# Key blocks of 32 on column tiles for two products of a gated scan

## What is computed

```python
def step(S, xs):                      # per chunk of 64 tokens
    qc, kc, vc, bc = xs               # b: cumulative log of the forget gate f
    diff = bc[:, :, :, None, :] - bc[:, :, None, :, :]
    diff = jnp.where(causal[None, None, :, :, None], diff, -jnp.inf)
    A = jnp.einsum('bhtd,bhsd,bhtsd->bhts', qc, kc, jnp.exp(diff))
    o = (jnp.einsum('bhts,bhsv->bhtv', A, vc)
         + jnp.einsum('bhtd,bhdv->bhtv', qc * jnp.exp(bc), S))
    ...
```

## Time and profile before

| | before |
|---|---|
| median of three runs | 1464.66 us |
| the profiled execution | 1463.35 us |
| its span, first to last instruction | 1461.5 us |
| TensorE busy (matmuls) | 1430.2 us, 98% |
| VectorE busy | 873.5 us, 60% |
| ScalarE busy | 574.4 us, 39% |
| GpSimd busy | 0.2 us |
| DMA | 158.31 MB, 33% of 16 engines' span |

### The profile page before, as it was taken

One profiled execution on the slowest core, in us unless ns is written; L12 is line 12 of the kernel. 1 busy time (PEld: TensorE's weight loads), 2 busy tenths in 40 slices (PEclk: granted clock), 3 DMA queues, 4 the chain that ended last, 5 costly groups with the idle time before them and its releaser, 6 DMA issues.

```text
span 1461.5 us, 18543 instructions
## 1 busy us (share of the span) xinstructions
PE 1430.2 (98%) x7204; PEld 1194.5 (82%) x7204; DVE 873.5 (60%) x1720; ACT 574.4 (39%) x1075; POOL 0.2 (0%) x4
## 2 busy tenths in 40 slices
PE   4999999999999999999999999999999999999998
PEld 3788888988888888888888888888888888888886
DVE  7887776544333335756467434424778787787645
ACT  5423355422232334533333333423445544555441
POOL 0000000000000000000000000000000000000000
PEclk9999999999999999999999999999999999999999
DMA  8646542353333234123223333332222222222221
GB/s 331 225 170 222 180 137 74 126 202 92 96 101 96 92 101 144 32 99 117 85 87 107 99 98 101 101 96 77 73 73 68 63 73 73 73 73 61 84 72 59
DMA packets 43863, 158.31 MB, mean 108 GB/s; under 512 B 4864, under 2 KB 5248, under 8 KB 43776
## 3 DMA queue, kind: packets, MB, share of 16 engines
q1 hardware_dynamic: 43776, 157.12, 33.0%
HBM read 155.00 MB, written 2.10 MB: 107 GB/s over the span
## 4 chain that ended last, share of the span: by engine, by line
PE 95%; DVE 3%; DMA 1%; ACT 1%; issue 0%; SPq 0%; ACTq 0%; DVEq 0%
PE PS L498 29%; PE PS L500 29%; PE PS L499 29%; PE PS L782 1%; PE PS L834 1%; PE PS L793 1%; PE PS L494 1%; PE PS L838 1%; PE PS L828 1%; DVE RAW L951 1%; DMA X<-in_x 1%; PE PS L853 1%; PE PS L814 0%; DMA RAW<-in_ada 0%; DVE Z L951 0%
## 5 line engine op out<-in xcount | busy, mean ns | idle before, releaser
L498 PE MATMUL PS<-HH,WH 128*128 128x512 f32 (+1 forms) x1088 | 430.7, 396 | 0.0
L500 PE MATMUL PS<-HH,WL 128*128 128x512 f32 (+1 forms) x1088 | 418.4, 385 | 0.0
L499 PE MATMUL PS<-HL,WH 128*128 128x512 f32 (+1 forms) x1088 | 417.0, 383 | 0.0
L987 DVE TENSOR_TENSOR WL<-RAW,WH 128x1024 fp32r<-128x1024 f32 x219 | 266.1, 1219 | 70.3 <-ACT WH L1695 70.1
L1695 ACT ACTIVATE WH<-RAW 128x1024 fp32r<-128x1024 f32 x219 | 230.6, 1056 | 171.7 <-PE PS L500 138.0
L500 PEld LDWEIGHTS PS<-HH,WL 128*128 128x128 f32 x1088 | 204.4, 188 | 42.1
L498 PEld LDWEIGHTS PS<-HH,WH 128*128 128x128 f32 x1088 | 204.7, 188 | 36.9
L499 PEld LDWEIGHTS PS<-HL,WH 128*128 128x128 f32 x1088 | 205.0, 188 | 36.0
L498 PE MATMUL PS<-WH,ZH 128*128 128x512 f32 x400 | 155.9, 390 | 0.0
L500 PE MATMUL PS<-WH,ZL 128*128 128x512 f32 x400 | 155.6, 389 | 0.0
L499 PE MATMUL PS<-WL,ZH 128*128 128x512 f32 x400 | 155.6, 389 | 0.0
(11 more groups left out here) (262 smaller groups left out, 1764.8 us busy)
## 6 DMA issues: line engine op xcount, KB each, us to landing
RAW<-in_w_fc SPq DMA_DIRECT2D x64, 512.0 KB, 3.6
RAW<-in_hgrn_in SPq DMA_DIRECT2D x64, 512.0 KB, 3.5
RAW<-in_ada SPq DMA_DIRECT2D x43, 512.0 KB, 4.4
RAW<-in_pool_in SPq DMA_DIRECT2D x40, 512.0 KB, 3.6
RAW<-in_w_in SPq DMA_DIRECT2D x27, 512.0 KB, 4.5
RAW<-in_pool_out SPq DMA_DIRECT2D x16, 512.0 KB, 3.6
RAW<-in_hgrn_out SPq DMA_DIRECT2D x16, 512.0 KB, 3.5
RAW<-in_w_out SPq DMA_DIRECT2D x8, 512.0 KB, 3.8
```

Source lines behind the costliest of these rows:

```text
L498: e.matmul(out, wh, xh, start=first, stop=False)
L499: e.matmul(out, wh, xl, start=False, stop=False)
L500: return e.matmul(out, wl, xh, start=False, stop=last)
L987: e.tensor_tensor(lo, raw(i), hi.bitcast(F32), ALU.subtract).then_inc(taken.sem, taken(i))
```

## The change

The products of lines 782 and 793 are cut into 16 groups of 32 keys. Each group g is multiplied with the queries of its own 32 tokens alone, and its output goes to the partitions 32 (g mod 4) to 32 (g mod 4) + 31, that is to one of four column tiles of TensorE. For levels 0 and 8 the queries of a group stand together in t.qp, 32 and then 16, in all 48 columns, and go to columns 64 g to 64 g + 47 of the pair of banks; for level 16 there are 16 queries to a group. t.qp keeps its size of 768 columns, but is ordered by group. The counts of elements that VectorE handles stay; masks and their contents stay; the semaphore of bank 3 is raised at group 7, that of bank 4 at the last.

```diff
-        QP = [sb(f"QP{i}", [128, 4, 192]) for i in range(2)]
+        QP = [sb(f"QP{i}", [128, 16 * 48]) for i in range(2)]
...
-                for i, c in enumerate(blocks):
-                    m = e.matmul(PAIR[:, 256 * i:256 * i + 192], t.f[:, c], t.qp[:, i, :], start=True, stop=True)
-                    if i == 1:
+                for g in range(16):
+                    r = 32 * (g % 4)
+                    m = e.matmul(PAIR[r:r + 32, 64 * g:64 * g + 48], t.f[:, 32 * g:32 * g + 32],
+                                 t.qp[:, 48 * g:48 * g + 48], start=True, stop=True)
+                    if g == 7:
                         m.then_inc(banks.full[3], banks.fill(("level", h, 0), 3))
...
-                for i, c in enumerate(blocks):
-                    m = e.matmul(PS[b][:, 64 * i:64 * i + 64].rearrange("p (n l) -> p n l", l=16), t.k[:, c],
-                                 halves(t.q[:, c], 16)[1], start=True, stop=True)
+                for g in range(16):
+                    r = 32 * (g % 4)
+                    m = e.matmul(PS[b][r:r + 32, 16 * g:16 * g + 16], t.k[:, 32 * g:32 * g + 32],
+                                 t.q[:, 32 * g + 16:32 * g + 32], start=True, stop=True)
...
                 (q0, q1), (w0, w1), (i0, i1) = (
-                    [v.rearrange("p (i n) l -> p i n l", i=4) for v in halves(x, 4)]
+                    [v.rearrange("p (g n) l -> p g n l", g=16) for v in halves(x, 4)]
                     for x in (t.q, W[:, :], IW[:, :]))
-                p4 = t.qp[:, :, 0:128].rearrange("p i (n a l) -> p i n a l", a=2, l=4)
+                qp = t.qp.rearrange("p (g c) -> p g c", c=48)
+                p4 = qp[:, :, 0:32].rearrange("p g (n a l) -> p g n a l", a=2, l=4)
...
-                    return x.rearrange("p (i n o) -> p i n o", i=4, o=1).broadcast_to([128, 4, 8, 8])
-
-                p8 = t.qp[:, :, 0:128].rearrange("p i (n a l) -> p i n a l", a=2, l=8)
-                qv = t.q.rearrange("p (i n a l) -> p i n a l", i=4, a=2, l=8)
+                    return x.rearrange("p (g n o) -> p g n o", g=16, o=1).broadcast_to([128, 16, 2, 8])
+
+                p8 = qp[:, :, 0:32].rearrange("p g (n a l) -> p g n a l", a=2, l=8)
+                qv = t.q.rearrange("p (g n a l) -> p g n a l", g=16, a=2, l=8)
                 e.wait_ge(own.sem, own.of("q8", h))
-                e.tensor_tensor(t.qp[:, :, 128:192].rearrange("p i (n l) -> p i n l", l=8),
+                e.tensor_tensor(qp[:, :, 32:48].rearrange("p g (n l) -> p g n l", l=8),
                                 p8[:, :, :, 1, :], by_pair(t.q8), ALU.mult).then_inc(scaled.sem, scaled(h, 8))
...
-                e.copy_predicated(t.diag, MSK[:, 0:512].rearrange("p (i t) -> p i t", i=4),
-                                  four[:, :, 0:128]).then_inc(banks.free[3], 1)
+                e.copy_predicated(t.A.rearrange("p (g l) -> p g l", g=16),
+                                  MSK[:, 0:512].rearrange("p (g l) -> p g l", g=16),
+                                  pair[:, :, 0:32]).then_inc(banks.free[3], 1)
...
-                    MSK[:, 512:768].rearrange("p (i n l) -> p i n l", i=4, l=8),
-                    four[:, :, 128:192].rearrange("p i (n l) -> p i n l", l=8)).then_inc(banks.free[4], 1)
+                    MSK[:, 512:768].rearrange("p (g n l) -> p g n l", g=16, l=8),
+                    pair[:, :, 32:48].rearrange("p g (n l) -> p g n l", l=8)).then_inc(banks.free[4], 1)
```

More of the change, by code:

```diff
@@ L1546, in mixing @@
                 t = Head(h)
-                four = PAIR[:, :].rearrange("p (i t) -> p i t", i=4)
+                pair = PAIR[:, :].rearrange("p (g c) -> p g c", c=64)
                 b = level_bank(h, 16)
@@ L1550, in mixing @@
                 e.wait_ge(*banks.made(("level", h, 8)))
-                e.copy_predicated(t.diag, MSK[:, 0:512].rearrange("p (i t) -> p i t", i=4),
-                                  four[:, :, 0:128]).then_inc(banks.free[3], 1)
+                e.copy_predicated(t.A.rearrange("p (g l) -> p g l", g=16),
+                                  MSK[:, 0:512].rearrange("p (g l) -> p g l", g=16),
+                                  pair[:, :, 0:32]).then_inc(banks.free[3], 1)
                 e.wait_ge(*banks.taken(("level", h, 0)))
                 e.copy_predicated(
-                    t.diag.rearrange("p i (n a l) -> p i n a l", a=2, l=8)[:, :, :, 1, :],
-                    MSK[:, 512:768].rearrange("p (i n l) -> p i n l", i=4, l=8),
-                    four[:, :, 128:192].rearrange("p i (n l) -> p i n l", l=8)).then_inc(banks.free[4], 1)
+                    t.A.rearrange("p (g n a l) -> p g n a l", g=16, a=2, l=8)[:, :, :, 1, :],
+                    MSK[:, 512:768].rearrange("p (g n l) -> p g n l", g=16, l=8),
+                    pair[:, :, 32:48].rearrange("p g (n l) -> p g n l", l=8)).then_inc(banks.free[4], 1)
                 yield
```

## The result

The changed kernel takes 1449.61 us (median of four, 1448.74 to 1449.90), the kernel before 1464.58 us in the same comparison; the ratio is 0.9897 with a 95% interval of 0.9885 to 0.9909. The profiled execution took 1449.90 us, its span is 1448.0 us.

A forecast was written before the change was run, and what follows sets the result against it. TensorE's queue was taken as the bound; gains of 0.63 us (levels 0 and 8) and 0.31 us (level 16) in 16 heads make 15.0 us, from the median of 1464.66 to 1449.7 us, range 1446.5 to 1456.5.

The forecast's parts named there:

- TensorE's queue is the bound: In the scan, 1020.3 to 1375.5 us, TensorE is always busy, so time taken from its queue comes out of the kernel's.
- Levels 0 and 8, 1.14 us expected: Line 782's group, dense start to second dense start, falls from 1.77 to 1.14 us, a gain of 0.63 us a head.
- the 55 of the other end: Line 782's slow estimate: 55 ns a round, on the line between 804 and 814, a gain of 0.56 us a head.
- Level 16, 1.05 us expected: Line 793's group falls from 1.36 to 1.05 us, rounds set by the weight load at 32 ns; gain 0.31 a head.
- The half price that the queries alone would allow: Line 793's alternative: rounds set by the queries, steps half as long, a gain of 0.41 us a head.
- The switch is inside line 804's 0.92 us and is paid two times more: Around both edited groups: the tiling switch, paid two times more per head, is already counted in line 804's 0.92 us.
- VectorE's layout at nothing: VectorE lines 1513, 1514, 1532, 1551, 1554: splitting into 16 groups keeps element counts and costs nothing.
- VectorE's chain: 0.27 us to spare at line 804: VectorE's work from line 1551 to 1566 before line 804: spare 0.58 us, less line 793's 0.31, leaves 0.27.
- VectorE's chain did not take over: Rival at line 804: slower predicated copies make TensorE wait, 1.5 to 5 us given back, 1451 to 1455; chance 0.10.
- Supply: Rival in both edited groups: instructions arrive too slowly, second 16 passes at 35 ns, 1462.0 us, half way 1456; chance 0.10.
- No overlap: Rival in both edited groups: the four tiles run one after another, 12.5 us lost, 1477 us; chance 0.04.
- the last of the prediction's signs of being wrong: Between the groups: dense matmuls starting further apart than before the change would show the prediction wrong.

## Why the prediction was right

The forecast was 1449.7 us, in a range of 1446.5 to 1456.5; measured were 1449.61. Its steps, one by one:

- **TensorE's queue is the bound, and starts are what counts.** Held. The cover of the other engines stayed, and the gains of the two groups were 10.1 and 4.8 us when taken one at a time.
- **Levels 0 and 8, 1.14 us expected.** 1.13. A step of the rounds came out at 43 ns (0.34 us for eight rounds more in the run with twice the passes), and the first one at 67. The mean over the group's seven steps is 46 ns, the number taken, for the reason given, a longer first step; the 55 of the other end has that step averaged in over only three.
- **Level 16, 1.05 us expected.** 1.03. Its 32 passes of 16 queries span 0.45 - 0.185 = 0.265 us, seven steps of 35 ns on the mean, a first one of 53 and the others of 32: the load of 32 keys sets the pace. The half price that the queries alone would allow did not come. In the heads with transposes behind it the group goes from 1066.34 to 1067.45 = 1.11 us, 1.13 expected, 1.43 before. Two numbers of this step in the prediction are off without touching the forecast: line 793's 0.104 us a pass averages a first step of 0.055 and later ones of 0.112 us, and the gain at half the step would have been 0.42 to 0.44 us, not 0.41, by its own terms (seven steps of 16 to 18.5 ns and 20 ns against the 0.13 us of line 804), which moves the low end by 0.5 us at most.
- **The switch is inside line 804's 0.92 us and is paid two times more.** Held: the weight loads of lines 784 and 797 show the same idle time as line 808's 5.7 us (the waits of the weight loads: us in total, times, longest):

```profile
PEld PS L797 <- issue: 5.7, 16, 0.4
PEld PS L784 <- issue: 5.6, 16, 0.4
```

  The Trainium skill's sentence on it (TensorEngine Tiling, Key Properties: changing the tiling mode drains TensorE) agrees, and the run with both groups together puts the price of one such switch at 0.28 us.
- **VectorE's layout at nothing.** Held, by the three durations above, and no difference with 128 keys in the new layout.
- **VectorE's chain: 0.27 us to spare at line 804.** The place was right, the size by luck, since two errors offset each other. The gap between VectorE's last operation and the group is 0.41 us, not 0.27. VectorE's copy starts 0.34 us after the group's last pass, where it was 0.43, so it gains 0.09 us (the records, whose ends are modelled, have a pass at 0.21 us with 48 queries and 0.33 with 192). And the switch back now lies behind the last pass: the second dense start comes 0.47 us after it, 0.40 before, which delays TensorE's side by 0.08 us. Level 16 took 0.33 us off, not 0.31, and 0.58 - 0.33 + 0.09 + 0.08 is 0.42. But of a gap 0.14 us is needed for the signal, which the prediction did not subtract. So 0.27 us is indeed what added work can take, the number that the prediction called spare.
- **What was missed:** the wait for line 1472 behind the last head, 0.98 us for a step that took 0.31 before, so 0.7 us. I had followed the chains inside a head, which repeat, and not the one at the end of the loop, which VectorE enters with more work queued. Against it, the two groups' gain over 16 heads is about 15.3 us rather than 15.0, by their means over all heads (1.76 to 1.13 us and 1.36 to 1.03). The two leave 14.6 us, and the profiles have 14.7 from the first start of levels 0 and 8 to the kernel's last matmul (433.7 and 419.0 us). The two profiled executions differ by only 13.5 us, as the later start hides 1.3; the medians show 15.0. That the sum met the median to 0.1 us is thus partly luck; a run of this kernel doesn't tell 1 us.
- **Rivals.** VectorE's chain did not take over (it begins to with 0.34 us more, and does with 0.68). Supply: refuted by 64 passes at the same pace. No overlap: refuted, but the run with the tiles out of turn shows how near it lies: the same passes in another order cost 15.8 us by their starts, and the gain depends on the rotation `32 * (g % 4)`. The break-even named there, 25 to 30 ns a pass, is 24 ns by the prediction's own terms, (1.77 + 1.36 - 2 x 0.79)/64.

The rule of 25 ns between starts (Trainium skill, TensorE: Matmul & The Clock Gate, Part 1) does not hold for passes on different column tiles: 32 and 64 passes came at 11 ns each, 16-query ones at 8. On one tile the smallest step seen is 32 ns, which the rule allows.

## What to carry to other kernels

Where only a diagonal of a product is wanted, cut the stationary side to the blocks that are wanted and rotate them over the column tiles: the cost of a round goes with the longer of one tile's stationary and moving columns, and to that comes a fixed switch in and out (0.28 us here) that is worth sharing between neighbouring groups. Price such a group by starts, from the dense matmul ahead to the second behind, on a line that already has the form. Take gains of a few us from starts inside the edited stretch, and look at the granted clock before a difference outside of it is explained. Then look for the next thing late not only inside the loop but where the loop ends, since a shorter engine arrives there with the others' work still queued.

## What the runs showed of the hardware

- Passes on one column tile follow each other after 43 ns (48 queries, 32 keys) or 32 ns (16 or 32 queries, 32 keys); with the tiles in turn four run side by side, 11 and 8 ns a pass.
- Passes for a busy tile hold up the others only when many stand in a row for it: with four in a row 32 passes take 0.38 us instead of 0.34, with eight 0.92. One running and three waiting for each tile fits both orders tried within 6%, but was not tried on a third.
- Passes are begun out of the program's order: with the first four all for one tile, the first four starts lie 13 to 14 ns apart, while passes on one tile follow each other after 43 ns.
- A switch into column tiles and back costs about 0.28 us, and the operands of the first tiled group may become ready as late as 0.14 us before its start, after the last dense matmul has begun.
- TensorE's granted clock fell to its lower level at 45 to 47 us in seven of the fourteen profiles, after a wait of 2.8 us in the changed kernel's. Dense matmuls then start 0.43 us apart instead of 0.23, and the fall cost 1.5 us there.
- After one step of 0.34 us behind a group, dense matmuls start 0.23 us apart again whatever the form of the group, so the last of the prediction's signs of being wrong did not show.
